# Reordering the row work beside the RWKV projections: key row first and in its own buffer, next keys a step sooner, one table for exp and log

## The chip, the cores and the metric

The kernel runs on one core of one Trainium2 chip. The metric is the device time of one execution in microseconds, from its median over several executions. The engines are TensorE (PE in the profile), VectorE (DVE), ScalarE (ACT), GpSimd (POOL) and the sync engine (SP), which here only issues DMAs.

## The reference

The whole program is a stack of two models on 1024 tokens of width 1024: window attention, latent attention, retention with stick-breaking attention, and last an RWKV-7 mixer. The change lies in the projections of that last mixer. Cut to what matters:

```python
def rwkv7_mixer(hn, mu, w_in, ...):
    xx = token_shift(hn) - hn
    xs = hn[None] + xx[None] * mu[:, None, None, :]
    r, k, v, g = jnp.einsum('pbsd,pdf->pbsf', xs[:4], w_in)
    w_log = -softplus(-(w0 + tanh(xw @ w1) @ w2)) - 0.5
    decay = exp(-exp(w_log))
    a = sigmoid(a0 + (xa @ a1) @ a2)
    kk = (k * k_k).reshape(B, S, H, N)
    kk = kk / maximum(norm(kk, axis=-1), 1e-12)
    k = k * (1.0 + (a - 1.0) * k_a)
    # a scan over the tokens with r, decay, k, v, kk, a; later also
    bonus = sum(rh * kh * r_k, axis=-1, keepdims=True) * vh
```

The scan runs in chunks of 64 tokens, so the kernel first turns its rows into decayed ones: with L the running sum of log decays in a chunk, it needs r·exp(L), k·exp(-L), kk·a·exp(-L) and kk·exp(L before this token), beside the bonus sums.

## The kernel before

`rwkv_projections` makes the four products r, k, v, g as sixteen steps j = 0 to 15: four steps each for k, r, v and g, each step two tiles of 128 tokens. A step is one block product by a scheme with seven half-size multiplications (class `Seven`), so TensorE works through `pe_5`, `pe_6`, `pe_3`, `pe_7`, `pe_1` of the next step, `pe_4`, and `pe_2` of the next step. Before each of them the sums of its left factor (`pool_s1` to `pool_s4`, on GpSimd) must be there, and after them VectorE adds the parts: `p15`, `u2` (L1040, L1046) and the output blocks `c12` (L1051), `c22` (L1056), `c21` (L1060). `pe_3` waits for `p15`, `pe_4` waits for `c22`. VectorE also makes the mixed inputs of the step after the next in `mix`: one instruction of 2048 elements (L4137) and then eight of 256 elements (L4140). The next `p15` stands behind them in VectorE's queue.

Beside these products runs the row work of `ScanRows`, one tile of 128 tokens in each of the steps 5, 6, 8, 9, 10, 12, 13 and 14 (`STEP_OF`). Its buffers are one row tile each, 128 x 1024 in float32: `row_r`, `row_k`, `row_a`, `row_w` are loaded from HBM, and `kk`, `t1`, `upto`, `back` are made. There is one copy of each, so the load of the next tile waits until the last use of this one. For tile i:

- SP has loaded w, k, a and r. `pool_keys` (L3811, GpSimd) makes kk = k·k_k; ScalarE squares it into `back` (L3782), VectorE sums the squares by head (L3843) and floors them (L3845).
- TensorE sums the decays, `pe_decays` (L3774), right behind `pe_5`; it needs `row_w`. ScalarE makes `upto` = exp (L3791), and `back` = exp of the negative (L3795) from the banks after VectorE's `dve_before` (L3850).
- ScalarE makes `t1` = a - 1 (L3787), GpSimd multiplies it by k_a (L3816), VectorE makes the key (`dve_key`, L3861) and then the r row (L3868), both between its `c12` and its `c22`.
- ScalarE makes the reciprocal norm by log and exp (L3793, L3797) and scales kk by head (L3801), then exp of `row_w` (L3803). VectorE multiplies kk by a (`dve_normed`, L3855), the bonus rows (L3874) and their sums (L3876) before `c21` and `mix`.
- GpSimd, behind `pool_bonus` (L3821) and `pool_s3` (L987), makes the x row (L3827), the b row (L3832) and the k row (L3838), in this order. SP stores each and loads the next tile's row into the buffer: the x row's store (L3725) is followed by the load of `row_w` (L3700), the k row's store (L3742) by the loads of `row_k` (L3703) and `row_a` (L3708); the last one waits until the b row is stored.

GpSimd runs one step ahead: its iteration j works on the factors of step j while TensorE is in step j - 1, and the row work of a tile of step j - 1 is in it. Each engine's order is written out by hand; there is no planner.

Of the kernel before, what the change touches and what calls it, by code (L numbers as in the profile page):

```python
# [10 lines left out]
ACT = mybir.ActivationFunctionType  # L11
# [5 lines left out]
CTX_TILES, X_TILES = 2, 8  # L17
# [107 lines left out]
def one_table(act):  # L125

    act.preload_act_table_set("natural_log_exp_and_others")
# [3512 lines left out]
class ScanRows:  # L3640
# [95 lines left out]
    def sp_b_row(self, sp, i):  # L3736
        sp.wait_ge(self.q["b_row_made"], i + 1)
        sp.dma_start(self.raw[5][self.at(i), :], self.row_a).then_inc(self.q["b_stored"], 16)

    def sp_k_row(self, sp, i):  # L3740
        sp.wait_ge(self.q["k_row_made"], i + 1)
        sp.dma_start(self.raw[1][self.at(i), :], self.back).then_inc(self.q["k_stored"], 16)  # L3742
        if i + 1 < X_TILES:
            self.sp_load_k(sp, i + 1)
            self.sp_load_a(sp, i + 1)

# [30 lines left out]
    def act_rows(self, act, i):  # L3777
        q = self.q
        act.wait_ge(q["kk_made"], i + 1)
        if i:  # L3780
            act.wait_ge(q["k_stored"], i * 16)
        act.activation(self.back, self.kk, ACT.Square).then_inc(q["squared"], 1)  # L3782
        act.wait_ge(q["ones_made"], 1)
        act.wait_ge(q["a_in"], (i + 1) * 16)
        if i:
            act.wait_ge(q["key_made"], i)
        act.activation(self.t1, self.row_a, ACT.Identity, bias=self.minus_one[:, :]).then_inc(q["less_made"], 1)  # L3787
        act.wait_ge(q["L_made"], i + 1)
        if i:
            act.wait_ge(q["r_stored"], i * 16)  # L3790
        act.activation(self.upto, self.sum_banks, ACT.Exp).then_inc(q["upto_decayed"], 1)  # L3791
        act.wait_ge(q["sums_floored"], i + 1)
        act.activation(self.norm[:, :], self.norm[:, :], ACT.Ln).then_inc(q["ln_made"], 1)  # L3793
# [40 lines left out]
    def pool_k_row(self, pool, i):  # L3834
        q = self.q
        pool.wait_ge(q["key_made"], i + 1)
        pool.wait_ge(q["b_row_made"], i + 1)
        pool.tensor_tensor(self.back, self.row_k, self.back, ALU.mult).then_inc(q["k_row_made"], 1)  # L3838

# [39 lines left out]
def rwkv_projections(nc, core, a, raw, weights, room, scan, row_sums):  # L3879
# [3 lines left out]
    LO, PAIRS, NT = LORA, X_TILES // 2, X_TILES  # L3883
# [4 lines left out]
    with ExitStack() as mem:  # L3888
# [44 lines left out]
        with nc.Block() as block:  # L3933

            @block.sync
            def _(sp):
# [18 lines left out]
                for j in range(J):  # L3955
                    gated = stream(j) == G
# [20 lines left out]
                    for i, m in lows[3:5]:  # L3977
                        store_low(i, m)
                    if tile is not None:
                        scan.sp_x_row(sp, tile)  # L3980
                    store(j, *((silu21_made, q) if gated else (seven.c21_read, j + 1)), s21, 1, 0, stored21)
                    for i, m in lows[5:6]:
                        store_low(i, m)
                    if tile is not None:
                        scan.sp_r_row(sp, tile, stored_by_tile)
                        scan.sp_b_row(sp, tile)
                        scan.sp_k_row(sp, tile)
                    if j == 2:
# [13 lines left out]
            def _(pool):  # L4002
# [6 lines left out]
                for j in range(J):  # L4009
                    pa, pb = pair_set(j)  # L4010
                    tile = scan.tile_at(j - 1)
                    if tile is not None:
                        scan.pool_keys(pool, tile)
# [8 lines left out]
                    seven.pool_s3(pool, j, pa, pb)  # L4022
                    if tile is not None:
                        scan.pool_x_row(pool, tile)
                        scan.pool_b_row(pool, tile)
                        scan.pool_k_row(pool, tile)

            @block.scalar
            def _(act):
# [49 lines left out]
                for j in range(J):  # L4079
                    gated, last = stream(j) == G, j == J - 1  # L4080
                    lows = LOW_TILES.get(j, ())
                    fronts = [i for i in (EARLY + 2 * j, EARLY + 2 * j + 1) if i < NT]
                    tile = scan.tile_at(j)
                    if tile is not None:
                        scan.act_rows(act, tile)
# [1073 lines left out]
```

## Time and profile before

| | us |
|---|---|
| median of 3 runs | 3709.26 (3707.15 to 3713.65) |
| profiled execution: its own time | 3713.88 |
| profiled execution: span | 3712.1 |
| PE busy over the span | 3467.2 (93%) |
| DVE busy | 1865.9 (50%) |
| ACT busy | 1154.8 (31%) |
| POOL busy | 864.9 (23%) |
| steps 5 to 14 of the projections (2769.64 to 3061.14) | 291.50, of which PE busy 268.02 |

The profiled execution took 1.8 us more than its span; times inside the trace count from the start of the span. A busy share over the span tells little of the stretch in question: what counts there is where TensorE waits.

### The profile page before, as it was taken

Reading aid. Unit: us, or ns where it says so; the run is one execution under the profiler, and the core shown is the slowest. Engines: PE = TensorE matmul, PEld = TensorE weight load, DVE = VectorE, ACT = ScalarE, POOL = GpSimd, SP = SyncE. Lnnn points to the kernel's source line nnn. Section 1 sums busy time; section 2 is a strip of 40 time slices with the busy share of each in tenths; the row PEclk is TensorE's granted clock in tenths of the full one; section 3 lists DMA queues with packets and bytes.
Section 4 is the critical chain, followed back from the end, with each engine's and each line's share of the span. In section 5 each row is a group of like instructions: output and inputs, shape, how many; then the busy total and the mean of one; then the engine's idle time right before and its main releaser. Section 6 shows DMA issues by size and latency. Waiting matters only on the chain. (4 is left out here: it accounts for less than half of the span.)

```text
span 3712.1 us, 64726 instructions
## 1 busy us (share of the span) xinstructions
PE 3467.2 (93%) x27290; PEld 2028.3 (55%) x27290; DVE 1865.9 (50%) x2911; ACT 1154.8 (31%) x2214; POOL 864.9 (23%) x544
## 2 busy tenths in 40 slices
PE   8999999999998999899999999998899997887998
PEld 3447874445555777544455447444444335877543
DVE  3336652323218999631466228224658874665322
ACT  1127760102224555311311028112213352221124
POOL 0000003440000000242333210333126660333532
PEclk9999999999998999999999999999999998998999
DMA  6000013226235455510522020111264535443400
GB/s 244 29 23 2 2 45 127 88 71 173 77 102 143 126 134 133 196 46 17 181 81 80 0 91 2 68 46 18 89 235 174 201 135 155 118 113 82 165 12 40
DMA packets 312102, 358.43 MB, mean 97 GB/s; under 512 B 161540, under 2 KB 215028, under 8 KB 309126
## 3 DMA queue, kind: packets, MB, share of 16 engines
q1 hardware_dynamic: 311816, 354.30, 29.8%
q8 instruction: 218, 3.57, 0.4%
q14 instruction: 68, 0.56, 0.0%
HBM read 255.88 MB, written 98.29 MB: 95 GB/s over the span
## 5 line engine op out<-in xcount | busy, mean ns | idle before, releaser
L2200 DVE TENSOR_SCALAR_CACHE_REDUCE la_s<-psum 128x1280 f32<-128x1280 f32 x128 | 190.7, 1491 | 35.3 <-PE psum L2244 27.6
L2169 ACT ACTIVATE la_s<-la_s,la_negm 128x1280 f32<-128x1280 f32 x128 | 174.4, 1362 | 82.2 <-DVE la_s L2200 82.2
L970 POOL TENSOR_TENSOR lg_seven_s<-other_columns 128x512 f32<-128x512 f32 x4 | 5.1, 1264 | 732.3 <-POOLq L112 711.8
L991 PE MATMUL psum<-room,x_rows 128*128 128x512 f32 x320 | 145.6, 598 | 5.7 <-POOL x_rows L970 5.7
L970 POOL TENSOR_TENSOR wg_seven_s<-other_columns 128x512 f32<-128x512 f32 x5 | 6.3, 1268 | 592.3 <-POOLq L112 544.6
L835 DVE CUSTOM_DVE_ANT_0 wa_s<-psum,window_mask_rows 128x640 f32<-128x640 f32 (+1 forms) x128 | 100.6, 786 | 71.6 <-PE psum L890 71.6
L3328 POOL TENSOR_TENSOR x_rows<-x_rows,pg_g 128x512 f32<-128x512 f32 x56 | 84.0, 1500 | 153.7 <-DVE pg_g L3477 140.2
L991 PE MATMUL psum<-room,rp_seven_s 128*128 128x512 f32 x256 | 115.2, 593 | 3.2 <-DVE rp_seven_p L1040 3.2
L793 ACT ACTIVATE wa_s<-wa_s,wa_negm 128x640 f32<-128x640 f32 (+2 forms) x160 | 117.3, 742 | 0.4 <-DVE wa_negm L838 0.3
L991 PE MATMUL psum<-rp_t,rp_seven_s 128*128 128x512 f32 x256 | 117.0, 600 | 0.0
L991 PEld LDWEIGHTS psum<-room,x_rows 128*128 128x128 f32 x320 | 60.5, 192 | 77.8 <-issue 77.8
L786 ACT ACTIVATE wa_pT<-psum 128x512 f32<-128x512 f32 (+1 forms) x160 | 80.4, 552 | 64.0 <-PE psum L900 63.8
L890 PE MATMUL psum<-window_kT,window_qT 64*128 64x256 f32 (+1 forms) x800 | 95.6, 366 | 2.9 <-DVE wa_s L832 1.2
L2244 PE MATMUL psum<-first_weights,latent_qr 32*128 32x320 f32 x1024 | 94.3, 435 | 0.0
L927 PE MATMUL psum<-wa_pT,window_v 128*64 128x128 f32 x1344 | 91.5, 279 | 0.5 <-ACT wa_oT L808 0.2
L2208 DVE STREAM_TRANSPOSE la_pT<-la_s 128x1280 f32<-128x1280 f32 x64 | 90.1, 1474 | 0.0
L2208 DVE STREAM_TRANSPOSE x_rows<-la_s 128x1280 f32<-128x1280 f32 x64 | 90.1, 1473 | 0.0
L991 PE MATMUL psum<-rp_t,rp_mixed 128*128 128x512 f32 x128 | 70.0, 698 | 20.9 <-DVE x_rows L1056 20.9
L991 PE MATMUL psum<-pg_t,pg_seven_s 128*128 128x512 f32 x192 | 86.3, 592 | 0.0
L991 PEld LDWEIGHTS psum<-room,rp_seven_s 128*128 128x128 f32 x256 | 48.3, 190 | 64.2 <-issue 64.2
L900 PE MATMUL psum<-ident,wa_s 128*128 128x128 f32 x576 | 81.9, 283 | 0.3 <-ACT wa_s L793 0.3
L890 PEld LDWEIGHTS psum<-window_kT,window_qT 64*128 64x128 f32 x800 | 69.7, 187 | 22.4 <-issue 12.6
(719 smaller groups left out, 7947.4 us busy)
## 6 DMA issues: line engine op xcount, KB each, us to landing
x_rows<-rwkv_raw SPq DMA_DIRECT2D x40, 512.0 KB, 4.8
room<-rwkv_raw SPq DMA_DIRECT2D x33, 512.0 KB, 5.2
later_slot<-in_ada_w_dram SPq DMA_DIRECT2D x16, 1024.0 KB
rwkv_raw<-x_rows SPq DMA_DIRECT2D x64, 256.0 KB, 2.9
rwkv_raw<-x_rows SPq DMA_DIRECT2D x32, 512.0 KB, 4.2
room<-in_odd_w_in_dram SPq DMA_DIRECT2D x6, 2048.0 KB, 13.0
first_weights<-latent_v SPq DMA_DIRECT2D x32, 320.0 KB, 5.4
la_v<-latent_v SPq DMA_DIRECT2D x32, 320.0 KB, 5.5
```

The lines of the kernel that those rows point to most:

```text
L786: act.activation(pT[:, u % 2, b, :, :].rearrange("p t q -> p (t q)")[:, 0:n], pT_banks[b][:, 0:n], ACT.Copy).then_inc(pT_moved, 1)
L793: act.activation(s_sb[:, u % 2, b, 0:n], s_sb[:, u % 2, b, 0:n], ACT.Exp, scale=SCALE, bias=negm[:, par, k:k + 1], accum_out=total[:, par, ...
L835: dve.tensor_tensor_reduce(out=s_sb[:, u % 2, b, 0:n], in0=s_banks[b][:, 0:n], in1=mask[:, lo:lo + n], scale=1.0, scalar=NEG, op0=ALU.add, ...
L890: last = pe.matmul(s_banks[b][:, at:at + n * P], qT[rows, p, t * P:(t + 1) * P], kT[rows, p // 4, k * P:(k + n) * P], start=True, stop=True)
L900: last = pe.transpose(pT_banks[b][:, n * P:(n + 1) * P], s_sb[:, u % 2, b, n * P:(n + 1) * P], core.ident)
L927: last = pe.matmul(o_bank[rows, (p % 4) * P:(p % 4 + 1) * P], v[:, k, g * A_DIM:(g + 1) * A_DIM], pT[:, u % 2, b, n, :], start=(n == 0), s ...
L991: last = pe.matmul(bank, left[:, k, :], right[:, k, :], start=fresh and k == 0, stop=k == HK - 1, skip_group_check=True)
L2169: act.activation(s, s, ACT.Exp, scale=-1.0, bias=negm[:, u % RING:u % RING + 1], accum_out=total[:, head(u) % 2, tile(u):tile(u) + 1]).the ...
L2200: dve.tensor_scalar(by_lane(s_sb[:, u % RING, :]), by_lane(banks_of(scores_side(u)))[:, :, 0:SPAN], -SCALE, FAR, ALU.mult, ALU.min, accum_ ...
L2208: dve.transpose(pT[h % 2][:, t, :], s_sb[:, u % RING, :]).then_inc(turned, 1)
L2244: last = pe.matmul(core.banks(scores_side(u) * LANE_GROUPS + r)[:, 0:SPAN], left, right, start=(b == 0), stop=(b == NOPE_BLOCKS))
L3328: pool.tensor_tensor(rows, rows, g[:, :], ALU.add).then_inc(x_made, 1)
```

## The change

GpSimd makes the k row first, into `t1` instead of `back`, and then the x row and the b row; the multiplication kk = k·k_k of the next tile follows at the end of the same iteration, where it stood at the start of the next tile's. SP stores the k row and loads the next `row_k` ahead of the x row, once the bonus rows have been multiplied; the load of `row_a` follows the b row's store. ScalarE makes `upto` before `t1`, and `t1` now waits for the k row's store where the squares did. ScalarE loads one table set that has both exp and log ahead of the first tile and of the tiles in the gated steps.

```diff
     def sp_b_row(self, sp, i):
         sp.wait_ge(self.q["b_row_made"], i + 1)
         sp.dma_start(self.raw[5][self.at(i), :], self.row_a).then_inc(self.q["b_stored"], 16)
+        if i + 1 < X_TILES:
+            self.sp_load_a(sp, i + 1)
 
     def sp_k_row(self, sp, i):
         sp.wait_ge(self.q["k_row_made"], i + 1)
-        sp.dma_start(self.raw[1][self.at(i), :], self.back).then_inc(self.q["k_stored"], 16)
+        sp.dma_start(self.raw[1][self.at(i), :], self.t1).then_inc(self.q["k_stored"], 16)
         if i + 1 < X_TILES:
+            sp.wait_ge(self.q["bonus_rows"], i + 1)
             self.sp_load_k(sp, i + 1)
-            self.sp_load_a(sp, i + 1)
...
         act.wait_ge(q["kk_made"], i + 1)
-        if i:
-            act.wait_ge(q["k_stored"], i * 16)
         act.activation(self.back, self.kk, ACT.Square).then_inc(q["squared"], 1)
-        act.wait_ge(q["ones_made"], 1)
-        act.wait_ge(q["a_in"], (i + 1) * 16)
-        if i:
-            act.wait_ge(q["key_made"], i)
-        act.activation(self.t1, self.row_a, ACT.Identity, bias=self.minus_one[:, :]).then_inc(q["less_made"], 1)
         act.wait_ge(q["L_made"], i + 1)
         if i:
             act.wait_ge(q["r_stored"], i * 16)
         act.activation(self.upto, self.sum_banks, ACT.Exp).then_inc(q["upto_decayed"], 1)
+        act.wait_ge(q["ones_made"], 1)
+        act.wait_ge(q["a_in"], (i + 1) * 16)
+        if i:
+            act.wait_ge(q["k_stored"], i * 16)
+        act.activation(self.t1, self.row_a, ACT.Identity, bias=self.minus_one[:, :]).then_inc(q["less_made"], 1)
...
         pool.wait_ge(q["key_made"], i + 1)
-        pool.wait_ge(q["b_row_made"], i + 1)
-        pool.tensor_tensor(self.back, self.row_k, self.back, ALU.mult).then_inc(q["k_row_made"], 1)
+        pool.wait_ge(q["back_decayed"], i + 1)
+        pool.tensor_tensor(self.t1, self.row_k, self.back, ALU.mult).then_inc(q["k_row_made"], 1)
...
                     if tile is not None:
+                        scan.sp_k_row(sp, tile)
                         scan.sp_x_row(sp, tile)
...
                         scan.sp_b_row(sp, tile)
-                        scan.sp_k_row(sp, tile)
...
                     tile = scan.tile_at(j - 1)
-                    if tile is not None:
+                    if tile == 0:
                         scan.pool_keys(pool, tile)
...
                     if tile is not None:
+                        scan.pool_k_row(pool, tile)
                         scan.pool_x_row(pool, tile)
                         scan.pool_b_row(pool, tile)
-                        scan.pool_k_row(pool, tile)
+                        if tile + 1 < NT:
+                            scan.pool_keys(pool, tile + 1)
...
                     tile = scan.tile_at(j)
+                    if tile == 0 or tile is not None and gated:
+                        one_table(act)
                     if tile is not None:
                         scan.act_rows(act, tile)
```

## Rows read from the trace of the kernel before

**Rows 1.** Windows by step (us; PE, PEld, DVE, ACT, POOL busy; granted clock; DMA share; GB/s).
```profile
2769.64:2795.39 25.75, 25.75 (x62) 11.40 (x61) 19.04 (x22) 14.38 (x28) 18.36 (x9) 1.00 0.34 124
2795.39:2828.29 32.90, 28.15 (x61) 12.10 (x60) 25.41 (x23) 12.87 (x27) 22.74 (x11) 0.90 0.45 159
2828.29:2854.93 26.64, 24.54 (x57) 10.47 (x56) 23.15 (x19) 1.19 (x2) 14.29 (x7) 1.00 0.87 313
...
2880.68:2912.89 32.21, 28.88 (x61) 12.41 (x60) 25.84 (x23) 12.87 (x27) 23.36 (x12) 0.89 0.47 167
2912.89:2943.61 30.72, 27.72 (x62) 11.91 (x60) 24.74 (x23) 12.87 (x27) 21.80 (x10) 0.94 0.43 160
2943.61:2970.70 27.09, 24.54 (x58) 10.47 (x57) 23.60 (x19) 2.48 (x3) 14.74 (x7) 1.00 0.80 292
...
2996.45:3028.84 32.39, 28.98 (x61) 12.39 (x60) 24.78 (x24) 17.33 (x32) 22.37 (x11) 0.89 0.47 165
3028.84:3061.14 32.30, 27.98 (x62) 11.83 (x61) 21.91 (x21) 17.33 (x32) 21.79 (x11) 0.95 0.45 165
```

**Rows 2.** Timeline of TensorE, steps 6 and 7 (start us, us, instruction, idle before).
```profile
2798.82 1.88 PE L3774 MATMUL psum<-x_rows,rs_decay_upto 128*128 128x512 f32 x4
...
2810.84 3.60 PE L991 MATMUL psum<-first_weights,rp_mixed 128*128 128x512 f32 x8
2819.19 5.83 PE L991 MATMUL psum<-rp_t,rp_mixed 128*128 128x512 f32 x8 [4.75 <-DVE x_rows L1056]
...
2836.71 3.67 PE L991 MATMUL psum<-room,rp_seven_s 128*128 128x512 f32 x8 [1.39 <-DVE rp_seven_p L1040]
```

**Rows 3.** Timelines of GpSimd, ScalarE and VectorE, tile 1 in step 6.
```profile
2806.77 2.35 POOL L3811 TENSOR_TENSOR x_rows<-x_rows,rp_squares 128x1024 f32<-128x1024 f32 x1 [6.59 <-issue]
...
2811.32 2.35 POOL L3816 TENSOR_TENSOR x_rows<-x_rows,columns 128x1024 f32<-128x1024 f32 x1 [0.98 <-ACT x_rows L3787]
...
2810.11 1.13 ACT L3787 ACTIVATE x_rows<-x_rows,rs_minus_one 128x1024 f32<-128x1024 f32 x1
...
2817.32 1.21 DVE L3868 TENSOR_TENSOR x_rows<-x_rows 128x1024 f32<-128x1024 f32 x1
2818.45 0.68 DVE L1056 TENSOR_TENSOR x_rows<-psum,rp_seven_p 128x512 f32<-128x512 f32 x1
```

**Rows 4.** Timelines of VectorE and GpSimd, tile 0 in step 5.
```profile
2784.17 1.21 DVE L3868 TENSOR_TENSOR x_rows<-x_rows 128x1024 f32<-128x1024 f32 x1
...
2792.89 2.60 DVE L4137 TENSOR_TENSOR rp_mixed<-rp_hT 128x2048 f32<-128x2048 f32 x1
...
2790.00 3.34 POOL L3827 TENSOR_TENSOR x_rows<-x_rows 128x1024 f32<-128x1024 f32 x1
2793.30 4.39 POOL L3832 TENSOR_TENSOR x_rows<-x_rows 128x1024 f32<-128x1024 f32 x1
2797.83 2.34 POOL L3838 TENSOR_TENSOR x_rows<-x_rows 128x1024 f32<-128x1024 f32 x1
```

**Rows 5.** SP's timeline (DMA issues), and landings of L3725, L3700 and L3708.
```profile
2826.49 0.32 SPq L3725 DMA_DIRECT2D rwkv_raw<-x_rows  x1
...
2836.12 0.32 SPq L3708 DMA_DIRECT2D x_rows<-rwkv_raw  x1
...
DMA to landing us min/median/max: 2.6/2.9/2.9
...
DMA to landing us min/median/max: 3.8/4.7/4.8
...
DMA to landing us min/median/max: 4.1/4.2/6.0
```

**Rows 6.** VectorE's timeline, the mix in step 6 and what follows it.
```profile
2828.64 7.32 DVE L4140 SCALAR_TENSOR_TENSOR rp_mixed<-rp_mixed,rp_mu,rp_hT 128x256 f32<-128x256 f32 x8
2835.89 0.68 DVE L1040 TENSOR_TENSOR rp_seven_p<-psum,rp_seven_p 128x512 f32<-128x512 f32 x1
```

**Rows 7.** ScalarE's table loads of one line, grouped (count, us, mean ns).
```profile
L3793 ACT ACT_TABLE_LOAD x8 | 10.3, 1283 | 0.1
```

## The prediction, written before the changed kernel was run

> **What bounds the kernel now.** I read the windows by step first. A step of the products with row work costs 25.75 us when TensorE never waits, with PE busy equal to the window: step 5, granted clock 1.00 [rows 1]. It holds 60 matmuls, 56 for the seven products and 4 for the decay sums: 0.43 each, so 3.43 a product, 1.72 the decay sums and 24.0 a step without row work. The second tile of each run of neighbouring steps (steps 6, 9, 13) takes 32.90, 32.21 and 32.39 us, the third (steps 10, 14) 30.72 and 32.30 [rows 1]. That is 6.75 and 5.8 us over, 32 us in the five. Steps 7 and 11 have no tile and still take 26.64 and 27.09.
>
> TensorE's timeline says where. In step 6 it stops 4.75 us before `pe_4`, for c22 (L1056), and the eight matmuls behind the stop take 5.83 us instead of 3.60 [rows 2]; the window's granted clock is 0.90 [rows 1], a mix of the level of 2.4 GHz and of 1.2 GHz. So the stop costs 4.75 and then 2.2 more. Step 7's stop of 1.39 for `p15` [rows 2] is in a window at clock 1.00 [rows 1]: a short stop doesn't bring the slow stretch.
>
> Why c22 is late: GpSimd stands idle for 6.59 us before it multiplies the next keys at 2806.77; their load was issued behind the k row's store. ScalarE squares them and makes `t1` at 2810.11, VectorE goes through sums, `c12`, key and r row (L3868 from 2817.32), and c22 is made at 2818.45 + 0.68 [rows 3]. TensorE was ready for it at 2810.84 + 3.43 = 2814.3 [rows 2]. The chain begins with the k row, last of three multiplications on GpSimd.
>
> **How the three multiplications are spaced.** In tile 0 the r row ends at 2784.17 + 1.21 = 2785.38. The x row is done at 2793.34, the b row at 2797.69, the k row at 2800.17 [rows 4]: 8.0, 12.3 and 14.8 us after the r row. The middle one takes 4.39 because it was asked for at 2793.30, after L4137 had been asked for at 2792.89, and the two didn't run at the same time: L4137 ran to 2795.49, and only then came GpSimd's 2.2 us. The k row, with nothing of that kind ahead of it, takes 2.34. I take these as places in a queue that don't depend on which row is multiplied in them.
>
> The Trainium skill has a rule for this (SBUF — State Buffer, Who interferes with whom): a VectorE instruction with two inputs in SBUF and a GpSimd instruction that reads SBUF exclude each other for the whole instruction. By that rule the third term below stands as it is; if the two engines shared by halves and small pieces slipped through, that term would shrink towards nothing. This rule speaks against the change, since it puts one more multiplication beside the mix; the rows agree with it.
>
> **Part 1, the k row first.** The k row takes the first place, the x row the second (12.3 after the r row, 4.3 later than now), the b row the third. Behind the x row on SP stands its store and then the load of `row_w`, issued 0.4 later, which lands in 4.7 (3.8 to 4.8) [rows 5], 5.1 after the x row. Now that is 2793.34 + 5.1 = 2798.4, and TensorE wants the decay sums of tile 1 at 2798.82 [rows 2]: slack 0.4. After the change it is 2797.69 + 5.1 = 2802.8. TensorE stops 4.0 us before L3774, where it doesn't stop at all now, and everything behind it in its queue is late by that. A stop of this length lies between the 1.39 without and the 4.75 with a slow stretch; I count 2.2, as it is nearer the latter; 0 is the other end.
>
> **Part 2, the next keys sooner.** k is loaded 7 us sooner, and its multiplication follows the b row at once: GpSimd at about 2800.5 instead of 2806.77, so the squares are there before TensorE has made `u2`'s input. The wait behind L3811 goes. What is late next is row a. Its load waits for the b row's store, which is issued behind x store, w load, the c21 store, r store and r load. From the x row's store to that load now passes 2836.12 - 2826.49 = 9.6 us, and it lands 4.2 later [rows 5]; the same queue stands there after the change, without the k pair. So row a lands at 2797.7 + 13.8 = 2811.5. Then `t1` 1.1, L3816 2.35 [rows 3], and from the end of L3816 to the end of the r row 2818.53 - 2813.67 = 4.9 [rows 3]: the r row ends at 2820.0 and c22 at 2820.6. Now it is 2819.13. So c22 isn't sooner; the gain of this part is taken by the a row.
>
> **Part 3, the tables.** Two loads of 1.28 us a tile go: the one for the log at L3793 [rows 7], and the one that brings exp back at L3795. That is 2.57 a tile, 20.5 in eight; the loads that `one_table` adds stand where L3791's stood. Of what is behind them, VectorE needs L3801 for L3855, and that stands behind c22, the product's wait. So I value them at nothing, with VectorE's work up to c22 as the cover; without it they would give back at most 2.57 a tile. The Trainium skill (ScalarE: Activation LUTs, What ACT_TABLE_LOAD costs) gives 2.66 us for a switch with its drain; no row here shows the drain, and by that figure ScalarE would win 2 x 2.66 x 8 = 43 us instead of 20.5, the sum staying the same.
>
> **The sum.**
> - Second tiles (6, 9, 13): 25.75 + 4.0 + 2.2 = 31.95; `pe_4` is then wanted at 2820.5, c22 comes at 2820.6, so 32.1. Now 32.5 on average. -0.4 x 3 = -1.
> - Third tiles (10, 14): taking tile 1's times as the pattern, r row 2820.0 + 12.3 + 5.1 = 2837.4 for the load of w, and TensorE wants it at 2820.7 + 3 x 3.43 = 2831.0. Stop 6.4, slow stretch 2.2: 34.4 against 31.5. +2.9 x 2 = +6.
> - Steps 7 and 11: `p15` waits in VectorE's queue for the mix. Now L4140 starts at 2828.64 and takes 7.32 [rows 6], with two of GpSimd's multiplications in it. After the change the third place ends at 2820.0 + 14.8 = 2834.8, and the next keys follow (they need the x row stored, 2.9 after its issue [rows 5], 2835.3) until 2837.6; then 2.6 us of pieces remain, as behind the k row now (2818.53 + 14.8 = 2833.3, to 2835.96). `p15` is made at 2840.9; `pe_3` wants it at 2820.7 + 4 x 3.43 = 2834.4. Stop 6.4 and slow stretch 2.2, against 1.39 and 1.8 now: +7.0 x 2 = +14. Bounds: 0 if the pieces pass between, +9 each with a longer slow stretch.
>
> Together +18.5. The profiled execution's own time is 3713.9, so 3732.4; it stands 4.6 above the median of the runs, so 3728 for a median. This case's own range is 3718 (no slow stretch behind the 4.0) to 3738.
>
> **Rivals.**
> - *The mix isn't held up.* Small pieces pass between GpSimd's multiplications, or the keys' one waits long enough. For it: step 7 stops only 1.39 now with two of them beside it. Against: L4140 takes 7.32 for eight pieces, and the b row's multiplication stretched to 4.39 beside the large one [rows 4]. Then the third term is nothing and the sum +4.5: 3714, no change that can be told.
> - *The x row isn't late*, so that w is there in time (the other side). This is decided at L3700: the load has to be issued no more than 0.4 us later than now. It would hold if the k row fitted into idle time of GpSimd before 2790.00. Against it: `pool_bonus` and `pool_s3` stand ahead of it in the queue, and the first needs the r row, 2785.38 [rows 4]. Price: c22 at 2816.1 for row a against 2814.3 wanted, a stop of 1.8 with no slow stretch: 27.6 for second tiles (-4.9 x 3), some 28 for third ones (-3.5 x 2), but the mix costs +6.1 x 2. Sum -9.6: 3700.
> - *Row a is later still.* Its landing goes to 6.0 at most [rows 5], and the b store may take longer among its neighbours. Some 2 to 4 us more in each of five steps and a second slow stretch: +15 on top, 3743.
> - The change doesn't do what it says: excluded nearly, since the order of each queue is the order of the code.
>
> **How the numbers follow.** This kernel's measurement can tell about 0.2%, 7.4 us, from no change. Forecast 0.62, row a later 0.08, mix not held up 0.15, x row in time 0.15. Slower is 0.70, same 0.15, faster 0.15. The range 3698 to 3738 takes in the second rival's time and the forecast's own range, and leaves out the lower half of that rival and the late row a, under 0.2.
>
> **What the profile of the changed kernel would show.** TensorE's stop before `pe_4` for L1056 gone or under 1 us in steps 6, 9, 10, 13, 14, and in its place a stop before L3774 for the DMA of `row_w`, near 4 us in second tiles and 6 in third ones. L3811 right behind L3832, 6 us sooner. In steps 7 and 11 a stop for L1040 of 6 us, with L4140 near 10 us for its eight. No table load but L127's and those of the silu. Wrong would be: L3774 with no stop (the x row's place was not 12.3), or c22 made before 2817 (row a faster), or L4140 still at 7.3.

## The result, and the profile after

The changed kernel takes 3725.94 us, median of 6 runs (3723.10 to 3735.48), beside 3710.09 (3706.85 to 3713.65, 6 runs) for the kernel before on the same chip: a ratio of 1.0042, 95% interval 1.0030 to 1.0054. It is slower, by 15.8 us. The profiled execution's own time is 3727.69 us (span 3725.9), 13.8 more than the one before.

The windows by step of the changed kernel, cut and read as [rows 1]:

```profile
2768.49:2794.24 25.75, 25.75 (x61) 11.40 (x60) 19.58 (x22) 11.70 (x26) 18.36 (x9) 1.00 0.34 126
2794.24:2825.96 31.72, 27.88 (x61) 11.81 (x60) 26.04 (x23) 10.53 (x25) 21.58 (x10) 0.95 0.44 151
2825.96:2858.93 32.97, 26.57 (x57) 11.27 (x56) 25.89 (x19) 1.19 (x2) 14.56 (x8) 0.90 0.75 264
...
2884.68:2917.17 32.49, 28.55 (x61) 12.26 (x60) 26.25 (x23) 10.52 (x25) 21.22 (x11) 0.89 0.44 147
2917.17:2951.39 34.22, 28.46 (x61) 12.26 (x60) 28.12 (x23) 10.52 (x25) 23.18 (x11) 0.90 0.45 154
2951.39:2984.53 33.14, 27.26 (x58) 11.53 (x56) 25.37 (x19) 2.48 (x3) 14.39 (x7) 0.90 0.68 245
...
3010.28:3043.45 33.17, 29.24 (x61) 12.32 (x60) 26.62 (x23) 14.87 (x30) 22.05 (x11) 0.90 0.42 146
3043.45:3077.76 34.31, 29.04 (x62) 12.32 (x61) 27.05 (x22) 14.15 (x30) 22.84 (x10) 0.90 0.45 153
```

Steps 5 to 14 last from 2768.49 to 3077.76, 309.27 us; before, from 2769.64 to 3061.14, 291.50 [rows 1]: +17.8. The second tiles (steps 6, 9, 13) go from 97.50 to 97.38 in sum, the third ones (10, 14) from 63.02 to 68.53, and steps 7 and 11, which have no tile of their own, from 53.73 to 66.11; their granted clock was 1.00 and is 0.90. What lies ahead of step 5 is 1.15 shorter and what lies behind step 14 is 2.8 shorter: 17.8 - 1.15 - 2.8 is the 13.8 of the spans.

TensorE's timeline in the changed kernel, steps 6, 7 and 10, read as [rows 2]. The decay sums stand at L3776 now.

```profile
2801.67 3.63 PE L3776 MATMUL psum<-x_rows,rs_decay_upto 128*128 128x512 f32 x4 [3.84 <-issue]
2805.10 3.66 PE L991 MATMUL psum<-rp_t,rp_seven_s 128*128 128x512 f32 x8
...
2818.99 3.70 PE L991 MATMUL psum<-rp_t,rp_mixed 128*128 128x512 f32 x8
...
2838.67 5.70 PE L991 MATMUL psum<-room,rp_seven_s 128*128 128x512 f32 x8 [5.68 <-DVE rp_seven_p L1040]
...
2926.53 3.75 PE L3776 MATMUL psum<-x_rows,rs_decay_upto 128*128 128x512 f32 x4 [5.76 <-issue]
```

The 4.75 us in front of `pe_4` for c22 [rows 2] are gone: the matmuls of 2818.99 follow without a gap. A stop before the decay sums stands in their place, 3.84 in step 6 and 5.76 in step 10. It is put down to "issue", with no releaser shown. It is the wait for `row_w`: the load is issued at 2796.92 (below) and lands in 4.6 us (median of L3700), which comes to 2801.5, and L3776 begins at 2801.67. In step 7 the stop for `p15` is 5.68 where it was 1.39, and the eight matmuls behind it take 5.70 instead of 3.67. The waits from 2760 to 3105 us say the same in three lines (line, what it waited for, us in total, times, longest):

```profile
PE psum L3776 <- issue: 22.5, 5, 5.8
PE psum L991 <- DVE rp_seven_p L1040: 10.8, 2, 5.7
PE psum L991 <- DVE x_rows L1056: 2.3, 3, 0.8
```

GpSimd's and VectorE's timelines in the changed kernel, from tile 0's r row in step 5 to the mix of step 6:

```profile
2783.03 1.21 DVE L3868 TENSOR_TENSOR x_rows<-x_rows 128x1024 f32<-128x1024 f32 x1
...
2791.74 2.59 DVE L4141 TENSOR_TENSOR rp_mixed<-rp_hT 128x2048 f32<-128x2048 f32 x1
...
2816.05 2.29 DVE L3868 TENSOR_TENSOR x_rows<-x_rows 128x1024 f32<-128x1024 f32 x1
2818.26 0.68 DVE L1056 TENSOR_TENSOR x_rows<-psum,rp_seven_p 128x512 f32<-128x512 f32 x1
...
2828.47 9.46 DVE L4144 SCALAR_TENSOR_TENSOR rp_mixed<-rp_mixed,rp_mu,rp_hT 128x256 f32<-128x256 f32 x8
2837.84 0.68 DVE L1040 TENSOR_TENSOR rp_seven_p<-psum,rp_seven_p 128x512 f32<-128x512 f32 x1
...
2788.85 3.33 POOL L3838 TENSOR_TENSOR x_rows<-x_rows 128x1024 f32<-128x1024 f32 x1
2792.14 4.39 POOL L3827 TENSOR_TENSOR x_rows<-x_rows 128x1024 f32<-128x1024 f32 x1
2796.50 2.52 POOL L3832 TENSOR_TENSOR x_rows<-x_rows 128x1024 f32<-128x1024 f32 x1
2799.62 2.34 POOL L3811 TENSOR_TENSOR x_rows<-x_rows,rp_squares 128x1024 f32<-128x1024 f32 x1 [0.61 <-DMA rwkv_raw<-x_rows]
```

The r row ends at 2784.24. The k row (L3838) is done 7.9 us later, the x row (L3827) 12.3, the b row (L3832) 14.8: the same three places as in [rows 4], with the rows exchanged, and the 4.39 has stayed with the second place, not with the b row. The next keys (L3811) follow at 2799.62. The mix of step 6, with the x row, the b row and the next keys beside it, takes 9.46 for its eight pieces, where it took 7.32 with two multiplications beside it [rows 6]. Tile 1's r row ends at 2818.34 and its c22 is made at 2818.94, 0.05 us before `pe_4` begins at 2818.99: c22 is only just in time.

SP's issues of the same stretch, and ScalarE's `t1` for tile 1, in the changed kernel:

```profile
2796.56 0.32 SPq L3725 DMA_DIRECT2D rwkv_raw<-x_rows  x1
2796.92 0.43 SPq L3700 DMA_DIRECT2D x_rows<-rwkv_raw  x1
...
2799.32 1.56 SPq L3738 DMA_DIRECT2D rwkv_raw<-x_rows  x1
2806.01 0.32 SPq L3708 DMA_DIRECT2D x_rows<-rwkv_raw  x1
...
2810.23 1.15 ACT L3791 ACTIVATE x_rows<-x_rows,rs_minus_one 128x1024 f32<-128x1024 f32 x1 [3.87 <-DMA x_rows<-rwkv_raw]
```

The load of w (L3700) goes out at 2796.92 and the load of row a (L3708) at 2806.01, 9.45 behind the x row's store; it waits there for the b row's store (L3738) to land. ScalarE has stood idle for 3.87 us when row a comes, at 2810.2.

### The profile page after: what moved, and what is told of

It is laid out like the page before. It is cut to its first block and busy times, and to the rows that moved or that the text cites. A ratio compares the mean times of both kernels' runs of the same rounds, so it can differ in the third digit from the quotient of the medians.

```text
span 3725.9 us, 64703 instructions
## 1 busy us (share of the span) xinstructions
PE 3472.5 (93%) x27290; PEld 2026.5 (54%) x27290; DVE 1882.9 (51%) x2911; ACT 1135.2 (30%) x2198; POOL 866.8 (23%) x544
## 5 line engine op out<-in xcount | busy, mean ns | idle before, releaser
L4144 DVE SCALAR_TENSOR_TENSOR rp_mixed<-rp_mixed,rp_mu,rp_hT 128x256 f32<-128x256 f32 x128 | 95.4, 816 | 0.6
L991 PEld LDWEIGHTS psum<-rp_t,rp_seven_s 128*128 128x128 f32 x256 | 51.0, 201 | 65.4 <-issue 65.4
```

The costliest lines, as they stand in the source:

```text
L991: last = pe.matmul(bank, left[:, k, :], right[:, k, :], start=fresh and k == 0, stop=k == HK - 1, skip_group_check=True)
L4144: end = dve.scalar_tensor_tensor(out[:, k, :], out[:, k, :], mu[:, stream(j), k:k + 1], h_at(i, 2)[:, k, :], ALU.mult, ALU.add)
```

## The experiments

Ratios are to the kernel before, run on the same chip in each case. "Steps" is the sum of steps 5 to 14 in the profiled execution, from its windows; in brackets the second tiles, the third ones, and steps 7 with 11.

| kernel | median us (runs) | ratio, 95% interval | steps, us |
|---|---|---|---|
| before | 3710.09 (6) | | 291.50 (97.50, 63.02, 53.73) |
| the change | 3725.94 (6) | 1.0042, 1.0030 to 1.0054 | 309.27 (97.38, 68.53, 66.11) |
| e1_keys_back | 3728.88 (4) | 1.0044, 1.0028 to 1.0061 | 301.42 (98.92, 67.64, 57.61) |
| e2_x_first | 3719.87 (10) | 1.0022, 1.0010 to 1.0033 | 301.09 (103.22, 68.18, 52.44) |
| e3_table_alone | 3707.57 (10) | 0.9988, 0.9977 to 0.9999 | 290.14 (94.20, 64.51, 54.18) |
| e4_all_free | 3705.45 (10) | 0.9983, 0.9971 to 0.9995 | 280.61 (83.60, 60.68, 59.08) |
| a1_change_again | 3726.35 (7) | 1.0044, 1.0027 to 1.0061 | 311.16 (99.25, 68.20, 66.46) |
| a2_keys_back_again | 3726.02 (8) | 1.0038, 1.0027 to 1.0049 | 303.21 (95.53, 68.50, 61.93) |
| e5_row_a_free | 3720.05 (10) | 1.0024, 1.0010 to 1.0037 | 302.46 (95.35, 64.80, 65.06) |
| e6_w_late_alone | 3719.97 (10) | 1.0020, 1.0009 to 1.0031 | 299.62 (98.06, 67.60, 56.71) |
| e7_less_first | 3701.85 (9) | 0.9979, 0.9968 to 0.9991 | 283.17 (83.97, 60.04, 61.91) |
| e8_all_free_again | 3704.09 (8) | 0.9982, 0.9970 to 0.9994 | 283.58 (86.76, 58.76, 60.82) |

**The next keys back at the start of the next iteration** (e1_keys_back), all else as changed:

```diff
                     tile = scan.tile_at(j - 1)
-                    if tile == 0:
+                    if tile is not None:
                         scan.pool_keys(pool, tile)
...
                         scan.pool_b_row(pool, tile)
-                        if tile + 1 < NT:
-                            scan.pool_keys(pool, tile + 1)
```

> The change, with the multiplication of the next keys put back to the start of the next tile's iteration on GpSimd. All else is as in the change. Theory (three causes: w late, row a late, the mix held up by one more multiplication): steps 7 and 11 lose one multiplication of 2.34 us beside the mix, so the stops for p15 before pe_3 (5.68 and 5.16 us) fall to about 3.3 and 2.8, with a slow stretch still behind at least one of them; the stops before the decay sums (3.8 to 5.8) stay. Sum -5 us against the change, ratio to before 1.003. Rival (the keys' multiplication sooner is harmless, the mix is held up by the x and b rows alone): the stops in steps 7 and 11 stay above 5, ratio 1.004. Second rival (the keys sooner is what saves the second tiles): L1056 stops come back in steps 6, 9, 10, 13, 14 and the ratio goes above 1.007.

VectorE's and GpSimd's timelines in this kernel (the mix is at L4142), steps 5 to 7, and TensorE's of step 7:

```profile
2797.53 9.39 DVE L4142 SCALAR_TENSOR_TENSOR rp_mixed<-rp_mixed,rp_mu,rp_hT 128x256 f32<-128x256 f32 x8
...
2831.97 7.31 DVE L4142 SCALAR_TENSOR_TENSOR rp_mixed<-rp_mixed,rp_mu,rp_hT 128x256 f32<-128x256 f32 x8
...
2802.84 2.61 POOL L3811 TENSOR_TENSOR x_rows<-x_rows,rp_squares 128x1024 f32<-128x1024 f32 x1 [0.66 <-DMA rwkv_raw<-x_rows]
...
2840.03 5.37 PE L991 MATMUL psum<-room,rp_seven_s 128*128 128x512 f32 x8 [2.91 <-DVE rp_seven_p L1040]
```

One kernel shows both lengths of the mix: 9.39 where the next keys are multiplied beside it, 7.31 where the next step has no tile and so no keys. The difference, 2.1 us, is near the 2.3 that such a multiplication takes by itself. The stops for `p15` fall from 5.68 and 5.16 to 2.91 and 2.49, those before L3776 stay (4.20, 3.89, 5.18, 3.83, 5.19), and steps 7 and 11 are 8.5 us shorter together, 5.4 by the stops and the rest by shorter slow stretches. That is the theory's picture, but the ratio isn't: 1.003 was expected, and 1.0044 measured, no less than the change's.

**The x row first, the k row second** (e2_x_first), on GpSimd and on SP, the keys still behind the b row:

```diff
                     if tile is not None:
-                        scan.sp_k_row(sp, tile)
                         scan.sp_x_row(sp, tile)
+                        scan.sp_k_row(sp, tile)
...
                     if tile is not None:
-                        scan.pool_k_row(pool, tile)
                         scan.pool_x_row(pool, tile)
+                        scan.pool_k_row(pool, tile)
```

> The change, with the x row again first on GpSimd and in SP's queue, the k row second, the b row third. So w is loaded as early as in the kernel before. Theory (w late and row a late bound the second tiles side by side): the stops before the decay sums go to under 0.5, and stops for c22 (L1056) of 4 to 5 us come in their place, because row a lands as late as in the change; second tiles stay at 32 to 33 us, third tiles fall to 32, sum -3 to -7 against the change, ratio 1.002 to 1.0035. Rival (w alone is what the change costs): no stop before the decay sums and none over 1 us for c22, second and third tiles near 26 to 28, 25 us or more gained on the change, ratio 0.997 or lower.

TensorE's, VectorE's and SP's timelines in this kernel, steps 5 to 7:

```profile
2819.66 6.35 PE L991 MATMUL psum<-rp_t,rp_mixed 128*128 128x512 f32 x8 [7.22 <-DVE x_rows L1056]
...
2793.59 7.32 DVE L4144 SCALAR_TENSOR_TENSOR rp_mixed<-rp_mixed,rp_mu,rp_hT 128x256 f32<-128x256 f32 x8
...
2791.44 0.32 SPq L3725 DMA_DIRECT2D rwkv_raw<-x_rows  x1
...
2806.68 0.32 SPq L3708 DMA_DIRECT2D x_rows<-rwkv_raw  x1
```

With w in time no stop before the decay sums is left, and c22 is late instead, by 7.22, 5.65, 5.82, 5.45 and 6.01 us: row a's load goes out 15.2 us behind the x row's store, still behind that of the b row, where it takes 9.6 in the kernel before [rows 5], since the b row is the third of the multiplications here and not the second. The keys' load stands behind the k row, so their multiplication (2801.93) comes when the mix of 2793.59 + 7.32 is done, and the stops for `p15` are 0.88 and 1.37. So two late rows, w and a, stand side by side, and taking one away uncovers the other: the second tiles are 5.8 us longer than the change's in sum and the third ones only 0.4 shorter, where the theory had the third ones at 32 us each. Half of the loss is gone all the same, and by the table all of that comes from steps 7 and 11 (66.11 to 52.44): the mix is 7.32 long with the keys out of it, and TensorE, slowed behind its stop for c22 (6.35 us for eight matmuls), wants `p15` later.

**The table alone** (e3_table_alone), on the kernel before:

```diff
                     tile = scan.tile_at(j)
+                    if tile == 0 or tile is not None and gated:
+                        one_table(act)
                     if tile is not None:
                         scan.act_rows(act, tile)
```

> The kernel before with only the one table for exp and log. Theory: ScalarE's table loads lie beside other work up to c22; 16 loads fewer, no stop of TensorE changes by more than 0.3 us, ratio 1.000 (0.999 to 1.001). Rival: the head scaling (L3801) ends 2.6 us sooner in the gated steps and with it the bonus rows and the x row, so third tiles gain: steps 13 and 14 each 1 to 2 us shorter, ratio 0.999.

The sixteen table loads are gone (ScalarE's busy time 1134.4 us against 1154.8, for 2198 instructions against 2214). The stops for c22 are 4.64, 3.39, 3.64, 3.45 and 3.71, where they were 4.75, 3.33, 3.00, 3.41 and 3.45, and those for `p15` 1.83 and 1.84 after 1.39 and 1.83; before the decay sums of steps 10 and 14 new ones of 0.34 and 0.93 appear. Some of them move by more than the 0.3 us that was expected at most, as stops also do between two executions of one kernel (1.61 and 3.08 for c22 in step 9 of e4 and e8); none gets shorter by more than 0.11. The steps are 1.4 us shorter in sum, which is less than two executions of the same kernel differ by (309.27 and 311.16 for the change). The ratio, 0.9988, has an interval that ends just below 1: the medians speak for a gain of 0.4 to 8.5 us, and the trace doesn't say where it would lie.

**Everything late made free** (e4_all_free), on the changed kernel: the order on GpSimd is x, k, b row; the b row is made in `back`, so that row a needn't wait for its store; SP takes the r row, x row, w, r, and then k and b; the keys are back in the next iteration.

```diff
     def sp_load_a(self, sp, i):
-        if i:
-            sp.wait_ge(self.q["b_stored"], i * 16)
...
-        sp.dma_start(self.raw[5][self.at(i), :], self.row_a).then_inc(self.q["b_stored"], 16)
+        sp.dma_start(self.raw[5][self.at(i), :], self.back).then_inc(self.q["b_stored"], 16)
...
         act.wait_ge(q["kk_made"], i + 1)
+        if i:
+            act.wait_ge(q["b_stored"], i * 16)
...
-        pool.tensor_tensor(self.row_a, self.row_a, self.back, ALU.mult).then_inc(q["b_row_made"], 1)
+        pool.tensor_tensor(self.back, self.row_a, self.back, ALU.mult).then_inc(q["b_row_made"], 1)
...
                     if tile is not None:
-                        scan.sp_k_row(sp, tile)
+                        scan.sp_r_row(sp, tile, stored_by_tile)
                         scan.sp_x_row(sp, tile)
+                        scan.sp_next_r(sp, tile, stored_by_tile)
```

> A version built on the theory. x row first, then k row into t1, b row last and into back, so that row a's load waits only for the b row's multiplication and not for its store; in SP's queue the r row's store goes ahead of the x row's store, the r load behind the w load, then c21's store, k store and load, b store and load; keys multiplied at the start of the next iteration. Theory: w on time (under 0.5 us before the decay sums in second tiles), row a lands at least 5 us sooner against TensorE than in the change, c22 stops fall to 1 to 2.5 us with no slow stretch, p15 stops in steps 7 and 11 of 1.5 to 3.5; second tiles 27 to 28.5 us, third tiles 27.5 to 30. Sum some 8 to 14 us less than before, ratio 0.9965 to 0.998. Rival (the sums of squares, through the late load of k, bound c22 as in the kernel before): c22 stops of 3 to 4 stay, ratio 0.999 to 1.001.

TensorE's timeline in this kernel, its stops in steps 6, 7 and 10, VectorE's from step 6, and the loads of w and a on SP:

```profile
2816.75 3.70 PE L991 MATMUL psum<-rp_t,rp_mixed 128*128 128x512 f32 x8 [1.74 <-DVE x_rows L1056]
2834.26 5.19 PE L991 MATMUL psum<-room,rp_seven_s 128*128 128x512 f32 x8 [3.52 <-DVE rp_seven_p L1040]
...
2913.13 1.96 PE L3776 MATMUL psum<-x_rows,rs_decay_upto 128*128 128x512 f32 x4 [2.14 <-issue]
...
2813.81 2.28 DVE L3870 TENSOR_TENSOR x_rows<-x_rows 128x1024 f32<-128x1024 f32 x1
...
2794.16 0.43 SPq L3700 DMA_DIRECT2D x_rows<-rwkv_raw  x1
...
2801.01 0.43 SPq L3706 DMA_DIRECT2D x_rows<-rwkv_raw  x1
```

Row a's load follows w's by 6.85 us instead of 9.1, the long stops become 1.6 to 1.8 for c22 in all five steps and some 2.3 before the decay sums in the third tiles. The ratio is 0.9983, faster than both kernels. Of the 34.0 us by which the kernel before is over ten steps of 25.75, 23.1 are left, 7.0 of them the two stops for `p15`. The second tiles win 13.9 us on the kernel before, and steps 7 and 11 lose 5.4: with the mix at 7.31 as before, `p15` is made 18.0 us behind the r row as before, but TensorE, with no slow stretch behind its stop for c22, wants it after 14.7 and not after 16.8. Which of this kernel's edits gives how much isn't shown.

**The change and e1 once more on one chip** (a1_change_again, a2_keys_back_again).

> The change itself, unchanged, once more, so that the two kernels after it have it on the same chip. Ratio to before 1.003 to 1.0054.

> The change with the multiplication of the next keys back at the start of the next tile's iteration, a second time. Its trace showed the stops for p15 at 2.9 and 2.5 us against 5.68 and 5.16, and steps 5 to 14 shorter by 7.9 us than the change's, while its median didn't tell. Theory: 5 to 8 us faster than the change on the same chip (ratio of the two 0.998). Rival: the gain in these steps is given back in other stages, the two medians within 2 us.

The change repeats: 1.0044, stops of 4.12, 3.91, 5.35, 3.96, 5.18 before L3776 and of 5.09 and 4.93 for `p15`. The second kernel is again 8 us shorter in these steps (303.21 against 311.16; stops for `p15` 3.52 and 3.38), and its median lies 0.3 us below the change's. Its steps 7 and 11 are 4.5 us shorter here and its second tiles 3.7, where in e1 the whole gain was in steps 7 and 11. Twice the ten steps are 8 us shorter, and twice the median doesn't show it: 5 to 8 us were expected, and the rival, two medians within 2 us, is what came.

**Row a alone made free** (e5_row_a_free): the changed kernel with the first four hunks of e4 as shown above, that is the b row in `back` and row a's load not waiting for its store.

> The change, with the b row made into back instead of row_a, so that row a is loaded as soon as the b row is multiplied; the squares of the next tile wait for the b row's store. Theory (w and row a bound the second tiles side by side, within 1 us): the stops before the decay sums stay at 3.8 in second tiles, so these don't move by more than 1 us; the r row comes about 3 us sooner against the step's end, so third tiles stop 2 to 3 less, and the mix begins sooner, so the stops in steps 7 and 11 fall by 2. Steps 5 to 14 together 7 to 11 us under the change, ratio to before 1.0015 to 1.0025. Rival (row a was the main cost): second tiles fall by over 3 us each too, ratio under 1.0005.

SP's load of row a and ScalarE's squares for tile 1 in this kernel, and TensorE's stops in steps 6, 10 and 7:

```profile
2803.61 0.50 SPq L3706 DMA_DIRECT2D x_rows<-rwkv_raw  x1
...
2810.07 1.06 ACT L3782 ACTIVATE x_rows<-x_rows 128x1024 f32<-128x1024 f32 x1 [12.42 <-DMA rwkv_raw<-x_rows]
...
2804.28 3.65 PE L3774 MATMUL psum<-x_rows,rs_decay_upto 128*128 128x512 f32 x4 [3.83 <-issue]
...
2927.09 3.57 PE L3774 MATMUL psum<-x_rows,rs_decay_upto 128*128 128x512 f32 x4 [3.86 <-issue]
...
2840.72 5.97 PE L991 MATMUL psum<-room,rp_seven_s 128*128 128x512 f32 x8 [5.32 <-DVE rp_seven_p L1040]
```

The stops of the second tiles stay at 3.7 to 4.0, since w is as late as it was; the third tiles fall by 3.7 us in sum (64.80 against 68.53), since the r row of the second tile, from which their places are counted, no longer waits as long for row a: in step 9 it ends 3.1 us before `pe_4` begins, where it was 1.2. Neither of the stops for `p15`, 5.32 and 3.86, falls by the 2 us that were expected. On the same chip the median is 6.3 us below the change's (3720.05 against 3726.35), though the two ratios' intervals overlap. The gain is bounded by two things. Row a's load goes out 4.4 us behind the x row's store instead of 9.45, but takes 6.4 us to land (5.6 to 7.6), where it took 4.1. And the squares, which go to `back`, now stand for the b row's store: ScalarE is idle for 12.42 us before them, and `t1` comes behind them.

**w late, alone** (e6_w_late_alone), on the kernel before:

```diff
         sp.dma_start(self.raw[4][self.at(i), :], self.kk).then_inc(self.q["x_stored"], 16)
-        if i + 1 < X_TILES:
-            self.sp_load_w(sp, i + 1)
...
         sp.dma_start(self.raw[5][self.at(i), :], self.row_a).then_inc(self.q["b_stored"], 16)
+        if i + 1 < X_TILES:
+            self.sp_load_w(sp, i + 1)
```

> The kernel before, with one edit: SP issues the load of row_w behind the b row's store instead of behind the x row's, some 4.5 us later. Theory: a stop of 4 to 5.5 us before the decay sums in steps 6, 9, 10, 13, 14 (L3774), and the stops for c22 there gone or under 1, since the late keys hide behind the new stop; so step lengths hardly move in second tiles (32 to 34 us) and third ones (32 to 34). Ratio 1.000 to 1.002. Rival (stops add up): both stops in each of the five steps, 25 us and more slower, ratio 1.007.

SP's, TensorE's and VectorE's timelines in this kernel, steps 5 to 7:

```profile
2793.13 0.32 SPq L3725 DMA_DIRECT2D rwkv_raw<-x_rows  x1
...
2797.85 0.43 SPq L3700 DMA_DIRECT2D x_rows<-rwkv_raw  x1
...
2802.96 3.46 PE L3774 MATMUL psum<-x_rows,rs_decay_upto 128*128 128x512 f32 x4 [4.20 <-issue]
...
2836.14 5.37 PE L991 MATMUL psum<-room,rp_seven_s 128*128 128x512 f32 x8 [2.26 <-DVE rp_seven_p L1040]
...
2828.08 7.31 DVE L4140 SCALAR_TENSOR_TENSOR rp_mixed<-rp_mixed,rp_mu,rp_hT 128x256 f32<-128x256 f32 x8
```

The load of w is 4.7 us behind the x row's store instead of 0.4 [rows 5], and TensorE stops before the decay sums, by 4.20, 5.04, 4.28, 4.61 and 3.99 us; the stops for c22 are gone. So a stop for w and one for c22 don't add: the first takes the place of the second. The kernel is 0.2% slower than before, half of what the change costs. The ten steps are 8.1 us longer than before, 0.6 in the second tiles, 4.6 in the third ones and 3.0 in steps 7 and 11, and that with the mix at 7.31.

**`t1` ahead of the squares** (e7_less_first) and **e4 once more** (e8_all_free_again), on one chip. The first is e4 with two moves: on ScalarE `t1` goes ahead of the squares, on GpSimd `pool_less` (L3818 there, the multiplication of `t1` by k_a) ahead of the first factor's sum `pool_s1`. The second move, against e4:

```diff
                     if tile is not None:
                         scan.pool_keys(pool, tile)
-                    pool.wait_ge(mix_made, j + 1)
-                    seven.pool_s1(pool, j, pb)
                     if tile is not None:
                         scan.pool_less(pool, tile)
+                    pool.wait_ge(mix_made, j + 1)
+                    seven.pool_s1(pool, j, pb)
```

> The version with all loads freed (x row first, k row into t1, b row last into back), and in it t1 = a - 1 ahead of the squares on ScalarE, and its multiplication by k_a ahead of the first factor's sum on GpSimd. In that version's trace t1 stood behind the squares and the exp (2808.01, row a had landed by 2805.6), and c22 was 1.75 us late. Theory: the key and the r row come 1.5 to 3 us sooner, c22's stops go to under 0.5, the x row and with it w come sooner, so third tiles' stop before the decay sums falls from 2.1 to under 1, and the mix with them, so that the stops of 3.5 in steps 7 and 11 fall to 2 to 3. Steps 5 to 14 from 280.6 to 264 to 274 us, ratio to before 0.993 to 0.997. Rival (the sums of squares bound c22, as they need the late keys): c22 stops stay at 1 to 2, steps 5 to 14 no shorter than 278.

> The version with all loads freed once more, beside the one with t1 first, with more rounds: ratio 0.997 to 0.999.

ScalarE's and VectorE's timelines in e7_less_first, step 6:

```profile
2804.31 1.15 ACT L3785 ACTIVATE x_rows<-x_rows,rs_minus_one 128x1024 f32<-128x1024 f32 x1 [9.55 <-DMA x_rows<-rwkv_raw]
2805.36 1.04 ACT L3789 ACTIVATE x_rows<-x_rows 128x1024 f32<-128x1024 f32 x1
...
2806.43 1.22 DVE L3845 TENSOR_REDUCE rs_norm<-x_rows 128x16 f32<-128x1024 f32 x1 [2.99 <-ACT x_rows L3789]
2811.55 2.29 DVE L3870 TENSOR_TENSOR x_rows<-x_rows 128x1024 f32<-128x1024 f32 x1
```

The steps take 283.17 us, those of e4 on this chip 283.58; the medians are 3701.85 and 3704.09, and their intervals lie over each other. The theory's 264 to 274 us were missed, and the rival came true: the stop for c22 stays at 1.3 to 2.4 in four of the five steps. VectorE waits 2.99 us for the squares, whose keys were loaded behind the k row's store, and then L3870, the r row, takes 2.29 where it takes 1.21 with no multiplication of GpSimd beside it. The move took away a wait that another stood behind. e8 repeats e4, 0.9982.

## Why the prediction was right, step by step

- **w late.** The x row's place was the second, 12.3 us after the r row, as forecast. The stop before the decay sums was forecast at 4.0 in second tiles and 6.4 in third ones, and was 3.84, 3.94 and 3.78 in steps 6, 9 and 13 and 5.76 and 5.16 in steps 10 and 14. e6_w_late_alone shows it as a cause by itself: with nothing but w later by 4.3, stops of 4.0 to 5.0 come there, the third tiles grow by 4.6 us, and the kernel is 1.0020 of the one before. For the second tiles the sum said -1 and they gave -0.1, because what was added behind w was what c22's stop had cost.
- **Row a takes the gain of the sooner keys.** The squares were begun at 2802.0, long before they were wanted. `t1` began at 2810.23; the forecast for row a was 2811.5 on the clock of the trace before, in which step 5 begins 1.15 us later, so 2810.35 here: row a came within 0.1 us of its place. The time from the x row's store to the load was 9.45, forecast 9.6. c22 was forecast 0.1 us behind TensorE and came 0.05 ahead of it. e2_x_first shows that row a is a bound of its own (c22 late by 5.5 to 7.2 with w in time), e5_row_a_free that it works through the third tiles. This term, with w's in the third tiles, was forecast +6 and was +5.5.
- **The mix held up.** Forecast: L4140 near 10 us for its eight pieces, a stop of 6.4, +14. Measured: 9.46, stops of 5.68 and 5.16, +12.4. The name says too much, though: in step 7 `p15` is made 20.2 us behind the end of the r row instead of 18.0, which is the mix, and TensorE wants it 14.7 behind it instead of 16.8, since the slow stretch behind the stop for c22 is gone. Each is 2.1 us of the 4.3 by which this stop grows. The forecast's times have both, its words only the first. That the pieces don't pass between GpSimd's multiplications is what the rival of 3714 had denied, and it falls by rows: 3.26 us for eight pieces with no multiplication beside them (at 2862.61 in a1_change_again), 7.3 with two, 9.4 to 9.5 with three. The Trainium skill says it so (SBUF — State Buffer, Who interferes with whom): an instruction of VectorE with both inputs in SBUF and one of GpSimd that reads SBUF exclude each other for their whole length. These rows agree: each multiplication, 2.3 us long, adds 2.0 to 2.1.
- **The tables at nothing.** ScalarE's busy time fell by 19.6 us for 16 instructions less (1154.8 to 1135.2, 2214 to 2198), forecast 20.5. e3_table_alone has no long stop shortened, which agrees with a term of nothing. But its ratio, 0.9977 to 0.9999, speaks for a gain of 0.4 to 8.5 us, so that the term is nothing isn't shown, and a gain of some us from it may be hidden in the change's own loss. The 2.66 us that the Trainium skill gives for a switch with its drain (ScalarE: Activation LUTs, What ACT_TABLE_LOAD costs) isn't what the busy time shows, 1.2 a load, nor the timeline of the kernel before: the load at L3795 lasts from 2813.98 to 2815.26, and the next ACTIVATE begins at 2815.27.
- **The slow stretch.** I counted 2.2 us behind every long stop. The five windows with a tile are 2.1, 2.8, 2.7, 3.6 and 3.4 us longer than 25.75 and their stop (step 6: 31.72 - 25.75 - 3.84), at a granted clock of 0.89 to 0.95: the four decay sums take 3.63 to 3.75 instead of 1.88, and in some steps the eight matmuls behind them are still slowed. This term was 0.7 us too small on average, and made up for what the stops were too large. That the two errors cancel is luck.
- **The sum.** Forecast +18.5 in the ten steps, measured +17.8; the terms -0.1, +5.5 and +12.4 against -1, +6 and +14 (rounded). In the two larger ones the stops were too big (5.76 and 5.16 for 6.4 before the decay sums, 5.68 and 5.16 for 6.4 at `p15`), and the slow stretch was too small. Before the decay sums of step 10 the place of w was as forecast, 17.4 us behind the r row, but this r row (step 9) ended 1.2 us before `pe_4` began, where tile 1's pattern had 0.7. At `p15` of step 7 the pieces that were left behind the keys' multiplication took 1.9 us instead of 2.6. The remaining 4 us between the steps and the spans lie in parts of the program that the change doesn't touch, and are within the scatter of those parts (below). The medians differ by 15.8, near the forecast's 18.5.
- **The rivals.** "x row in time" (3700) was decided at L3700's issue, and its place was the forecast one. What it says comes true only with further edits: in e4_all_free w is in time for the second tiles and a is sooner, and it measures 0.9983. "Row a is later still" (3743) falls with `t1` at 2810.23, its forecast place.

**What stays open.** Without the keys beside the mix, the ten steps are 8 us shorter in two pairs of traces, and the ratios to the kernel before hardly are: 1.0044 against 1.0042, not taken side by side, and 1.0038 against 1.0044 on one chip. The intervals reach 0.11 to 0.17% to each side, 4 to 6 us, so part of the 8 may hide there. On one chip, e1 and e2 have ten steps of the same length (301.42 and 301.09 us) and medians 9.0 us apart. A single trace can't say why: what lies outside the ten steps took 3413 to 3429 us over all twelve traces, and between two executions of the same kernel it differed by 3.2 us (the change), 7.9 (e1's kernel) and 1.0 (e4's). Whether the shorter steps are paid for elsewhere, or the scatter covers them, these runs don't say.

So w late alone gives 8.1 of the 17.8 us in the trace and half of the loss in the medians (1.0020 against 1.0042). Freeing row a gives 6.3 us of median back, with intervals that overlap. The keys' multiplication beside the mix is worth 8 us in the trace and isn't shown in the medians. These prices can't be added up, since one stop hides another. The kernel before with nothing but the b row in its own buffer wasn't run, nor were e4's edits one by one.

## What to carry to other kernels

When one producer is moved ahead in a shared queue, price the consumers of what it displaces: here a row moved from the third place to the first made two others 4.3 and 2.5 us later, and behind one of them stood a load with 0.4 us of slack. A sooner start gained nothing here while the chain's other input came through a buffer that must be stored before it is loaded again; look for that store first (e5 frees that buffer, e4 the order as well). When a stop is taken away, look for the wait that it hid: in e2 it was row a behind w, in e4 `p15` behind c22. Count a long multiplication of GpSimd as time taken from VectorE's small pieces, nearly one for one: here 2.1 us of mix for 2.3 of multiplication.

## What was not expected of the hardware

- **What a short stop costs isn't a function of its length.** Stops of TensorE of up to 1.84 us were never followed by slowed matmuls (3.6 to 3.7 us for eight). One of 2.26 (e6, step 7) was followed by 5.37 for eight, and one of 2.25 in the same kernel (step 11) by 3.67; 3.52 in e4 by 5.19, and 3.53 in the same kernel by 3.67, in steps that do the same work. In these ten steps of the twelve traces every stop from 3.8 us on was followed by a slow stretch. In the windows that have one the granted clock is 0.86 to 0.95, between the levels of 2.4 and 1.2 GHz, and 1.00 in those without.
- **VectorE and GpSimd are served in the order in which they asked.** The second place of the three multiplications takes 4.39 or 4.40 us whichever row stands in it (x row in the change, k row in e2 and e4, b row before), each time with L4141 or its like asked for 0.4 us ahead of it. In step 6 of the change L4141 runs from 2825.83 to 2828.43, and the x row, asked for at 2826.24, ends at 2830.64, 2.2 us behind it. The first of the mix's small pieces is asked for at 2828.47, behind the x row, and takes 2.45 us, where all eight take 3.26 with nothing beside them.
- **Stores of the same 512 KB took very different times to land.** In the changed kernel SP's store of the b row took 3.7 to 8.2 us from issue to landing, 6.7 in the median, with the x row's store, w's load, the c21 store and the r row's store and load issued in the 3 us ahead of it; the x row's store, ahead of them all, took 2.6 to 3.5, 2.9 in the median. In the kernel before the b row's took 3.6 to 7.0, 5.3 in the median. That the neighbours are the reason is likely, but no run tests it.
